# A down product in seven block products, and a feed-forward front with the first half of the tokens ahead

## What is computed

```python
def _swiglu(x, w_gate, w_up, w_down):
    return (jax.nn.silu(x @ w_gate) * (x @ w_up)) @ w_down
h = h + 0.5 * _swiglu(_rmsnorm(h, norm), w_gate, w_up, w_down)   # D_FF = 2816
```

## Time and profile before

| | |
|---|---|
| median of 3 runs | 2445.79 us (2445.03 to 2451.75) |
| the profiled execution | 2445.71 us, span 2443.6 us |
| TensorE busy | 2227.4 us, 91% of the span, 10338 matmuls |
| VectorE busy | 1281.9 us, 52% |
| ScalarE busy | 863.9 us, 35% |
| GpSimd busy | 582.6 us, 24% |
| mean granted TensorE clock | 0.958 |

### The profile page before, as it was taken

One profiled execution on the slowest core, in us unless ns is written; L12 is line 12 of the kernel. 1 busy time (PEld: TensorE's weight loads), 2 busy tenths in 40 slices (PEclk: granted clock), 3 DMA queues, 4 the chain that ended last, 5 costly groups with the idle time before them and its releaser, 6 DMA issues. The chain is left out here.

```text
span 2443.6 us, 27322 instructions
## 1 busy us (share of the span) xinstructions
PE 2227.4 (91%) x10338; PEld 1846.6 (76%) x10338; DVE 1281.9 (52%) x1944; ACT 863.9 (35%) x1396; POOL 582.6 (24%) x500
## 2 busy tenths in 40 slices
PE   3999999989996979998959998799599999999997
PEld 3878888878885878886837776577488888888886
DVE  7685555533435327952347777451755555543444
ACT  5423233322223233153137776321432323322232
POOL 4347777600000002220002221000533233310000
PEclk8999999999997999998979999899699999999999
DMA  2323232373112363322420000241222222246111
GB/s 100 101 91 102 89 112 97 101 285 103 48 35 93 114 104 131 102 78 71 127 73 6 4 6 1 95 177 39 95 87 92 81 87 69 90 182 224 50 53 67
DMA packets 169729, 223.63 MB, mean 92 GB/s; under 512 B 32064, under 2 KB 121664, under 8 KB 169088
## 3 DMA queue, kind: packets, MB, share of 16 engines
q1 hardware_dynamic: 169600, 221.90, 28.1%
HBM read 162.58 MB, written 59.28 MB: 91 GB/s over the span
## 5 line engine op out<-in xcount | busy, mean ns | idle before, releaser
L48 PE MATMUL psum<-f_B_hi,f_A_hi 128*128 128x512 f32 x1232 | 483.5, 392 | 1.4 <-ACT rows L879 1.1
L50 PE MATMUL psum<-f_B_hi,f_A_lo 128*128 128x512 f32 x1232 | 479.8, 389 | 0.0
L49 PE MATMUL psum<-f_B_lo,f_A_hi 128*128 128x512 f32 x1232 | 479.5, 389 | 0.0
L48 PE MATMUL psum<-f_wd_hi,f_hh 128*128 128x512 f32 x704 | 274.8, 390 | 8.0 <-DVE f_hh L979 8.0
L49 PE MATMUL psum<-f_wd_lo,f_hh 128*128 128x512 f32 x704 | 274.4, 390 | 0.0
L50 PE MATMUL psum<-f_wd_hi,f_hh 128*128 128x512 f32 x704 | 274.4, 390 | 0.0
L48 PEld LDWEIGHTS psum<-f_B_hi,f_A_hi 128*128 128x128 f32 x1232 | 231.3, 188 | 50.0 <-issue 2.8
L50 PEld LDWEIGHTS psum<-f_B_hi,f_A_lo 128*128 128x128 f32 x1232 | 231.2, 188 | 48.7
L49 PEld LDWEIGHTS psum<-f_B_lo,f_A_hi 128*128 128x128 f32 x1232 | 231.4, 188 | 46.9
L977 DVE TENSOR_TENSOR f_wd_lo<-f_wd_raw,f_wd_hi 128x1024 fp32r<-128x1024 f32 x88 | 107.8, 1225 | 301.0 <-ACT f_wd_hi L898 301.0
L898 ACT CAST f_wd_hi<-f_wd_raw 128x1024 fp32r<-128x1024 f32 x88 | 92.8, 1055 | 352.2 <-PE psum L50 324.1
(11 more groups left out here) (306 smaller groups left out, 4064.0 us busy)
## 6 DMA issues: line engine op xcount, KB each, us to landing
f_raw<-ffn_w_gate SPq DMA_DIRECT2D x22, 1024.0 KB, 5.4
f_raw<-ffn_w_up SPq DMA_DIRECT2D x22, 1024.0 KB, 5.5
hidden<-rows SPq DMA_DIRECT2D x22, 1024.0 KB, 6.2
f_h_raw<-hidden SPq DMA_DIRECT2D x88, 256.0 KB, 2.7
f_wd_raw<-ffn_w_down SPq DMA_DIRECT2D x44, 512.0 KB, 14.3
rows<-x SPq DMA_DIRECT2D x16, 512.0 KB, 7.8
kept<-rows SPq DMA_DIRECT2D x2, 4096.0 KB, 15.0
ga_raw<-w_in SPq DMA_DIRECT2D x16, 512.0 KB, 4.5
```

Of the source, the lines that this page charges most:

```text
L48: pe.matmul(out, lhs_hi, rhs_hi, start=first, stop=False, skip_group_check=go_on)
L49: pe.matmul(out, lhs_hi, rhs_lo, start=False, stop=False, skip_group_check=go_on)
L50: return pe.matmul(out, lhs_lo, rhs_hi, start=False, stop=last, skip_group_check=go_on)
```

## The change

**Down stage.** The 2x2 block scheme is used here too: the pair is now tiles k and k+11, the weights of a pair are four blocks of 128x512 (`wd_block`), and there are seven rounds q of 11 units v = 11q+k. A unit is one product of 12 matmuls, so 77 units of 12 in place of 44 of 24. ScalarE casts 128x512 of `hh` and of `wd` per unit, VectorE subtracts both. The weight sums are made in place in `wd_raw` by VectorE during rounds 0 to 3 (`combine(q, k)`). The hidden sums are made by VectorE after each pair of matrices (`pair_sum`, four of 128x512: two after the up matrix, two in slots 0 and 1 of the next gate matrix; all four at once after the last pair), and seven blocks of `hidden` are stored by three transfers (seven blocks of 256 KB). Three results are kept in SBUF (`keep`, ScalarE), the others are added by VectorE straight from PSUM (`evict`), and seven small groups of adds (`add_u1` to `add_w_low`) spread them over `rows`.

**Front.** Tiles 0 to 3 are normalised first, in place in `rows`; their two plain blocks are turned and split (`turn_lows`). Then TensorE alternates: one of the products (0,0), (0,2), (1,0), (1,2), written (n,q), and one round of `turn_sums` (the five other blocks of one pair of tiles). `T` has two buffers. In the second FFN the residual is stored tile by tile and `scaled(m)` waits for the store of its tile. GpSimd no longer makes low parts.

**Order.** The weights of a matrix come in two transfers of 512 KB. Eight `h_raw` and the first four `wd_raw` loads stand ahead of the last `Tables` chunk; `Tables` slots of the chunks move later by one.

```diff
-            yield from self.until("pe", self.CHUNK_AT + 7 * ch + 6)
+            yield from self.until("pe", self.CHUNK_AT + 7 * ch + 7)
...
-            yield from self.until("dve", self.CHUNK_AT + 7 * ch + 7)
+            yield from self.until("dve", self.CHUNK_AT + 7 * ch + 8)
...
+EARLY = ((0, 0), (0, 2), (1, 0), (1, 2), (0, 1), (0, 3), (0, 4), (0, 5), (0, 6), (1, 1), (1, 3), (1, 4), (1, 5), (1, 6))
+WD_BLOCKS = ((0, 0), (0, 0), (0, 1), (0, 0), (0, 0), (1, 0), (1, 1))
...
-        UNITS = 2 * FT
+        UNITS = PRODUCTS * PAIRS
...
+            def store_pair(p):
+                sp.wait_ge(s_h, p + 1)
+                sp.dma_start(hidden[p, 0, 0:3].rearrange("q f s -> f q s"), h[:, 0:3]).then_inc(s_hout, 16)
+                sp.wait_ge(s_hs, 4 * p + 3)
+                sp.dma_start(hidden[p, 1, 1:4].rearrange("q f s -> f q s"), g[:, 1:4]).then_inc(s_gout, 16)
+                sp.wait_ge(s_hs, 4 * p + 4)
+                sp.dma_start(hidden[p, 0, 3], h[:, 3]).then_inc(s_hout, 16)
...
+            store_pair(PAIRS - 1)
+            for v in range(8, 12):
+                sp.wait_ge(s_dlo, 2 * (v - 7))
+                if v == PAIRS - 1:
+                    sp.wait_ge(s_hout, 32 * PAIRS)
+                    sp.wait_ge(s_gout, 16 * PAIRS)
+                load_unit(v)
             for m in range(ST):
                 sp.dma_start(rows[:, m, :], residual[m * P:(m + 1) * P, :]).then_inc(s_res, 16)
...
-            for u in range(8, UNITS):
-                sp.wait_ge(s_dlo, 2 * (u - 7))
-                load_unit(u)
+            for v in range(12, UNITS):
+                sp.wait_ge(s_dlo, 2 * (v - 7))
+                load_unit(v)
...
+                    if p and not j and q < 2:
+                        pair_sum(p - 1, q + 2)
                     tables_on(n, q)
                 if j:
                     dve.wait_ge(s_grest, p + 1)
                     dve.wait_ge(s_c12, n + 1)
                     dve.tensor_tensor(h[:, 1:4], h[:, 1:4], g[:, 1:4], ALU.mult).then_inc(s_h, 1)
+                    dve.wait_ge(s_h, p + 1)
+                    for i in range(2 if p + 1 < PAIRS else 4):
+                        pair_sum(p, i)
...
+            for v in range(UNITS):
+                q, k = v // PAIRS, v % PAIRS
+                if q >= 4 and k < QUAD:
+                    evict(q - 1, k)
+                if v:
+                    unit_low(v + 1)
+                if q < COMBINING:
+                    combine(q, k)
+                if q == 2 and 4 <= k < 8:
+                    add_u1(k - 4)
...
+            for m in range(QUAD):
+                turn_lows(m)
+            for m in range(QUAD):
+                first_product(*EARLY[m])
+                turn_sums(m)
```

More of the change, by code:

```diff
@@ L537, in scalar @@
         for ch in range(self.CHUNKS):
[L538 removed]
+            yield from self.until("act", self.CHUNK_AT + 7 * ch + 8)
             act.wait_ge(s["xt"], ch + 1)
@@ L837, in _, with square, squares, lows_high @@
         def _(act):
[L838 to L849, removed]
+            def square(m):
+                if x is not None:
+                    act.wait_ge(s_x[m], 16)
+                if m:
+                    act.wait_ge(s_sq, m)
+                act.activation(dump[:], rows[:, m, :], ACT.Square, accum_out=stat[:, 0, m:m + 1]).then_inc(s_sq, 1)
+            def squares(i):
+                square(2 * i)
+                square(2 * i + 1)
+                norm.root(act, i, slice(2 * i, 2 * i + 2))
+            def lows_high(m):
+                for i, q in enumerate(LOW_BLOCKS):
+                    act.wait_ge(s_tr, low_turned(m, i))
+                    act.copy(B_hi[:, q, :, tile(m)], blocks(LOW_BANKS[m][i])).then_inc(s_bhi, 1)
+            def sums_high(m):
+                if m == 0:
+                    act.wait_ge(s_sq, ST)
+                for i, q in enumerate(SUM_BLOCKS):
+                    act.wait_ge(s_tr, sum_turned(m, i))
+                    act.copy(B_hi[:, q, :, tile(m)], blocks(q)).then_inc(s_bhi, 1)
+            def first_copy(j):
+                act.wait_ge(s_mm, place(j, 0) + 1)
+                act.copy(t1_of(j), bank(banks[j][0])).then_inc(s_t1, 1)
             def high(n, q):
@@ L999, in _ @@
+            tables_on = beside(dve, "dve")
+            normalised(0)
+            normalised(1)
+            lows_low(0)
+            lows_low(1)
+            low(0, 0)
+            low(0, 2)
+            normalised(2)
+            lows_low(2)
+            lows_low(3)
+            normalised(3)
+            low(1, 0)
+            sums_low(0)
+            low(1, 2)
+            sums_low(1)
+            sums_low(2)
+            sums_low(3)
+            for q in (1, 3, 4, 5, 6):
                 low(0, q)
@@ L1048, in final_row, with into @@
-            def final_row(m):
-                dve.scalar_tensor_tensor(out=rows[:, m, :], in0=rows[:, m, :], scalar=stat[:, 3, m:m + 1], in1=fgain[:],
+            def into(out, src, done, round_, i):
+                if round_:
+                    dve.wait_ge(done, (round_ - 1) * QUAD + i + 1)
+                dve.scalar_tensor_tensor(out=out, in0=src, scalar=0.5, in1=out, op0=ALU.mult, op1=ALU.add).then_inc(done, 1)
+            low_left, low_right = (lambda i: rows[:, i, left]), (lambda i: rows[:, i, right])
@@ L1050, in final_row @@
+            def final_row(i):
+                m = FINAL[i]
+                dve.scalar_tensor_tensor(out=rows[:, m, :], in0=rows[:, m, :], scalar=stat[:, 3, i:i + 1], in1=fgain[:],
                                          op0=ALU.mult, op1=ALU.mult).then_inc(s_y, 1)
@@ L1070, in _ @@
-                add(6)
+                final_row(3)
+            for i in range(QUAD):
+                evict(PRODUCTS - 1, i)
+            if finish:
                 final_var(1)
-                add(7)
                 last.inverse(dve, 1, FGROUPS[1])
@@ L1079, in _ @@
                 final_row(7)
-            else:
-                for m in range(QUAD, ST):
-                    add(m)
         @block.gpsimd
```

521 lines of the change are left out of this document (308 added, 213 removed).

## The result

| | before | after |
|---|---|---|
| median | 2445.91 us (4 runs) | 2414.89 us (2413.12 to 2419.49, 4 runs) |
| ratio, 95% interval | | 0.987 (0.9852 to 0.9888) |
| profiled execution, its span | 2445.71, 2443.6 us | 2413.12, 2411.3 us |

A forecast was written before the change was run, and what follows sets the result against it. TensorE, 91% busy, was taken to bound the kernel. Terms from -59.8 us for removed matmuls to +12.3 for new waits summed to -61.3, from 2445.71 to 2384 us; own range 2373 to 2396, with rivals 2362 to 2410.

The forecast's parts named there:

- the matrix stage: First FFN's gate/up matrices: pair sums on VectorE make t2 and the table pieces late; +4 us (0 to +12).
- The front: Start of each FFN: as long as before, but four products done inside it; -11.4 us first FFN, -8.9 second.
- The waits of the down stage: Start of each down stage: new TensorE waits at units 2, 8, 12 and slow clock; +9.9 us first FFN, +12.3 second.
- Matmuls: Down stages of both FFNs: 264 fewer matmuls at 0.2267 us each, -59.8 us, if a unit is readied in 2.72.
- the stall: First unit of the first FFN's down stage: TensorE's 8.0 us wait and the slow clock behind it go; -9.5 us.
- the tail: Last norm: last scaling ends later, +2.6 us, and -0.5 at the first FFN's end; +2.1 in all.
- The small adds: Down stage, VectorE additions with both inputs in SBUF: about 0.69 us for 512, taken from the final scaling's row.
- The Trainium skill's rule: Two SBUF sources that are not bf16 halve VectorE's throughput; small adds would then cost some 4 to 5 us per FFN.
- the front gives nothing: Start of each FFN: each product between turns delays the turn, at half clock 5.1 us; +20, 2404 us, chance 0.12.
- the VectorE rival: Down stage, rounds 0 to 3: VectorE becomes the bound, 0.25 us over per unit; +22, 2406 us, chance 0.12.

## Where the prediction held and where it failed

**The step that failed** is the matrix stage: "Behind the fourth sum stand the table pieces that a TensorE table product in slot 2 awaits: 0.5 late, in eight gate matrices. **+4**". The right wait was named and mis-sized: 14.2 us in place of 4, 1.9 each in most matrices, and the stage lost 20 us, 4.2 of them before matrix 8. I costed the pair product at 1.75 and four sums at 0.69, as they run alone, though the same text knew that operations with both inputs in SBUF are slow beside GpSimd. It did not ask where GpSimd's chain would stand after the slots had moved: onto the product and two sums, 1.1 and 1.0 us. It also had t2 come 0.8 late at no cost: TensorE waited 3.3 us for t2, in matrices 2 and 4, where work of `Tables` stands in VectorE's list too.

**The front.** Its length was right within 0.8 us in the first FFN and 1.5 in the second. The two terms lost 9 of 20 us, nearly all behind it: the wait for t2 was costed at 0.9 twice per FFN, but in the first FFN (1,3) waited for two things that product (1,2) had covered, and in both (0,1) ran at the low clock (0.50 in its first 2 us). **The waits of the down stage** were right in place, cause and order; two terms were small by 1.4 and 3.6. Unit 12 began 2.9 and 2.6 later than forecast, the latter because SyncE's wait for the store left the queue empty, and the slow clock behind it cost 0.2 and 2.7 in place of 1.7 each. But both stages scatter: in the other runs that leave them alone the second took 222.2 to 224.3, which is 0.7 to 2.8 over the forecast, and the first 220.2 to 225.8, 0.9 to 6.5 over it. **Matmuls, the stall, the tail** came out within 0.6 us, and VectorE in rounds 0 to 3 was no bound: units are 2.72 apart from unit 13 on. The small adds took 0.685 for 128x512 with both inputs in SBUF (48 of them): no halving, so the row was the right source. The Trainium skill's rule that the prediction weighed (Vector Engine (DVE) Microarchitecture Reference, section 7) does not hold here. The rival "the front gives nothing" fails by its own run; its 2404 and the 2406 of the VectorE rival came closest to the time by chance of the sum, not by what they said would happen.

## What to carry over

When work is added to an engine's list, read what stands behind it in the list that another engine waits for, and cost the added operations by the durations that they have beside the other user of SBUF at the place where they will stand. A queue of loads should be in the order in which its data are due; here a mend of a wait upstream of a late load showed no gain. When an operation is taken out of a sequence, ask what it covered: here a table turn and an addition.

## What the runs showed of the hardware

VectorE with two SBUF inputs and GpSimd took turns by whole instructions: a pair product of 1.75 us took 2.84 behind a GpSimd sum that had started 0.5 us before it, and 1.75 when it started 0.16 ahead; a GpSimd sum of four elements took 1.72 behind it.
